# Two halves of weights at a time for keys, queries, both gates and the linear attention's output product

## The reference, cut to what matters

```
q, k, v, g, a_lr, p, bg = split(h @ w_in)     # h: 256 x 2048, for the latent tokens and for the context
o   = gla(q, k, v, decay(a_lr))               # 4 heads, forward and backward, chunks of 64
y1  = (rms(o) * gain * silu(g)) @ w_gla_out   # 256 x 2048 by 2048 x 2048
y2  = pool_branch(p) @ w_pool_out
x   = x + gt * ((sigmoid(bg1) * y1 + sigmoid(bg2) * y2) @ w_out)
```

## Time and profile before

| | |
|---|---|
| median of three runs | 2921.17 us |
| span of the profiled execution | 2918.2 us |
| its device time beside the span | not noted; the runs' median is 3.0 us above the span |
| TensorE busy | 2884.3 us (99%) |
| VectorE busy | 2112.9 us (72%) |
| ScalarE busy | 1444.3 us (49%) |
| TensorE's granted clock over the span | 0.996 of full |
| HBM read | 639.58 MB |

### The profile page before, as it was taken

One profiled execution on the slowest core, in us unless ns is written; L12 is line 12 of the kernel. 1 busy time (PEld: TensorE's weight loads), 2 busy tenths in 40 slices (PEclk: granted clock), 3 DMA queues, 4 the chain that ended last, 5 costly groups with the idle time before them and its releaser, 6 DMA issues.

```text
span 2918.2 us, 41112 instructions
## 1 busy us (share of the span) xinstructions
PE 2884.3 (99%) x16696; PEld 2513.1 (86%) x16696; DVE 2112.9 (72%) x2920; ACT 1444.3 (49%) x1929; POOL 10.8 (0%) x25
## 2 busy tenths in 40 slices
PE   8999999999999999999999999999999999999998
PEld 7889989888888888888878888888878888888887
DVE  6566767998998877699767665559987765555557
ACT  5455656544444445465445444544555444444444
POOL 0000000000000000000000000000000000000000
PEclk9999999999999999999999999999999999999999
DMA  7555345777777885587745455678647765555553
GB/s 272 188 213 191 131 169 207 267 267 260 268 267 262 317 304 203 200 296 279 270 167 199 175 184 197 219 262 292 241 155 284 291 220 188 188 188 189 187 188 114
DMA packets 108252, 653.78 MB, mean 224 GB/s; under 512 B 12032, under 2 KB 12288, under 8 KB 43936
## 3 DMA queue, kind: packets, MB, share of 16 engines
q1 hardware_dynamic: 100800, 625.93, 58.8%
q10 hardware_dynamic: 5328, 17.83, 1.5%
q0 software_dynamic: 1936, 7.41, 0.7%
HBM read 639.58 MB, written 11.53 MB: 223 GB/s over the span
## 4 chain that ended last, share of the span: by engine, by line
PE 95%; DVE 3%; ACT 1%; issue 1%; DMA 0%; SPq 0%; ACTq 0%; DVEq 0%
PE PS L527 51%; PE PS L538 27%; PE PS L613 3%; PE PS L615 3%; PE PS L623 3%; PE PS L522 1%; PE PS L524 1%; DVE RL L2162 1%; PE PS L870 1%; PE PS L1114 0%; PE PS L1128 0%; PE PS L645 0%; PE PS L839 0%; DVE X L3146 0%; PE PS L1046 0%
## 5 line engine op out<-in xcount | busy, mean ns | idle before, releaser
L2162 DVE TENSOR_TENSOR RL<-RW,RH 128x1024 fp32r<-128x1024 f32 x974 | 1171.1, 1221 | 424.8 <-ACT RH L1281 420.0
L1281 ACT ACTIVATE RH<-RW 128x1024 fp32r<-128x1024 f32 x974 | 1012.6, 1053 | 640.2 <-PE PS L527 499.5
L527 PE MATMUL PS<-A,RH 128*128 128x512 f32 x4272 | 1045.5, 394 | 13.3 <-ACT RH L1281 8.6
L527 PEld LDWEIGHTS PS<-A,RH 128*128 128x128 f32 x4272 | 782.5, 189 | 167.7 <-ACT RH L1281 8.9
L538 PEld LDWEIGHTS PS<-A,RL 128*128 128x128 f32 x4544 | 594.9, 191 | 28.3
L538 PE MATMUL PS<-A,RL 128*128 128x256 f32 x4544 | 606.6, 283 | 0.0
L527 PE MATMUL PS<-H,RH 128*128 128x512 f32 x2248 | 551.7, 396 | 0.0
L527 PEld LDWEIGHTS PS<-H,RH 128*128 128x128 f32 x2248 | 412.7, 188 | 86.1
L1288 ACT ACTIVATE LT<-PS 128x512 f32<-128x512 f32 x214 | 127.6, 596 | 473.6 <-PE PS L538 473.2
L538 PEld LDWEIGHTS PS<-H,RL 128*128 128x128 f32 x2304 | 296.1, 188 | 14.3
L538 PE MATMUL PS<-H,RL 128*128 128x256 f32 x2304 | 301.2, 282 | 0.0
(11 more groups left out here) (281 smaller groups left out, 1756.2 us busy)
## 6 DMA issues: line engine op xcount, KB each, us to landing
RW<-in_w_fin SPq DMA_DIRECT2D x88, 1024.0 KB, 4.8
G<-in_w_ada SPq DMA_DIRECT2D x160, 512.0 KB, 6.2
RW<-in_w_up SPq DMA_DIRECT2D x64, 1024.0 KB, 4.9
RW<-in_w_down SPq DMA_DIRECT2D x64, 1024.0 KB, 4.9
RW<-in_w_fout SPq DMA_DIRECT2D x44, 1024.0 KB, 4.8
RW<-in_w_v SPq DMA_DIRECT2D x32, 1024.0 KB, 4.8
RW<-in_w_bg SPq DMA_DIRECT2D x32, 1024.0 KB, 4.9
RW<-in_w_k SPq DMA_DIRECT2D x16, 1024.0 KB, 5.4
```

The costliest lines, as they stand in the source:

```text
L527: done = t.matmul(pair[mm][:, :], w, x2(4 * c + k)[0], start=c == 0 and k == 0, stop=False, skip_group_check=True)
L1281: a.activation(m.high(x), m.slot(j)[:, x % 2 * HC:x % 2 * HC + HC], ACT.Copy).then_inc(s["hi"], 1)
L2162: v.tensor_tensor(m.low(x), m.slot(j)[:, x % 2 * HC:x % 2 * HC + HC], m.high(x).bitcast(F32), ALU.subtract).then_inc(s["lo"], 1)
```

## The change

In four calls of `gemm` on the tensor engine, `paired=True` is added. No other engine's program and no data layout changes.

```
-    L.k2 = lambda use, b0, nb: gemm(nb, 4, A2, modulated(use) if use == b0 == 0 else nothing)
-    L.q2 = lambda: gemm(4, 4, A2, modulated(1), zipped=True)
+    L.k2 = lambda use, b0, nb: gemm(nb, 4, A2, modulated(use) if use == b0 == 0 else nothing, paired=True)
+    L.q2 = lambda: gemm(4, 4, A2, modulated(1), zipped=True, paired=True)
...
-    L.bg2 = lambda: gemm(4, 4, A2, nothing)
+    L.bg2 = lambda: gemm(4, 4, A2, nothing, paired=True)
...
-    L.gout = lambda: gemm(8, 4, H2, lambda c: t.wait_ge(s["gl"], c + 1))
+    L.gout = lambda: gemm(8, 4, H2, lambda c: t.wait_ge(s["gl"], c + 1), paired=True)
```

## The result

The kernel after takes 2925.39 us (median of 20 runs, 2923.64 to 2927.42), the one before 2920.62 us in the 20 runs beside it (2919.69 to 2921.69). The ratio is 1.0017, 95% interval 1.0011 to 1.0023: +4.8 us. The slowdown is less than the 0.2% that the prediction set as its bound for the same, but the interval doesn't reach 1: twenty runs beside twenty do tell 0.17% from nothing, where the prediction said that a measurement couldn't. The forecast was 2925.0 us.

What follows compares the result with a forecast made beforehand. TensorE, busy 99% of the span, was taken as the bound. The terms -1.1 + 0 + 0.95 + 4.1 + 0 - 0.1 gave +3.8 us on a median of 2921.17: 2925.0 us, range 2920.3 to 2929.5.

Steps and rivals of the forecast that it cites:

- Part 1: Keys, queries and gates, A as moving operand: pairing saves 0.020 us a pair, -1.1 us for 56 pairs.
- the order would cost nothing: Rival, all four products: pairs save nothing, waits stay; +4.9 us, 2926.1 us, chance 0.08.
- Part 2: gout's 16 pairs, H as moving operand: the order alone changes 0 us, bounds -0.3 and +0.1 us.
- Part 3: Queries' start: the second half's wait for ScalarE's copy grows by a half's narrow part, +0.95 us, bounds 0 and +1.6.
- Part 4: gout beside the pool: B directly follows A and waits for ScalarE's copy; +1.0 us a window, +4.1 us for four.
- The clock is no further price: TensorE's added waits: no extra cost from the clock, since it was 1.00 over the stretch with the 1.6 us wait.
- Part 5: Heads: some steps come a half, 2.8 us, later; one return to the product less in the fourth head, -0.1 us.
- the tight place: Fourth head's output, whose norm must be done before the transposes: nothing gained or lost, bounds 0 and +0.4 us.
- Part 6: Weights feeding the pairs: wanted 0.94 us sooner; narrowest behind gout's gate reload, 2.3 us of cover left, cost 0.
- ScalarE late in the pool: Rival, pool: ScalarE not idle when A's bank is full; +4.2 us (2929.2) or +6.6 us (2931.6), chance 0.10.
- The reload: Rival, gout's gate reload: it outlasts its cover and TensorE loses 2 us or so; 2927 to 2931 us, chance 0.04.
- The wait in the pool: Rival, pool: no wait, as A and B aren't side by side or the copy is early; 2920.3 us, chance 0.08.

Runs made afterwards that it cites:

- e8: Against the kernel before: keys and gates paired, queries paired from their second pair on, gout single; 2919.35 us against 2920.43, ratio 0.9997.
- e7: The kernel before with 120 pairs of other products (both MLPs and g2) unpaired; 2922.77 us against 2920.43, ratio 1.0007.
- e4: The kernel after with the eight wide matmuls of the queries' first half issued twice; 2924.67 us against 2920.30 for the kernel before, ratio 1.0015.
- e5: The kernel before with seven of eight narrow matmuls of the queries' first half left out; 2921.99 us against 2920.43, ratio 1.0003.
- e9: The kernel before with seven of eight wide and seven of eight narrow matmuls of the queries' first half left out; 2923.06 us against 2920.38, ratio 1.0008.
- e10: The kernel before with four of eight wide and seven of eight narrow matmuls of the queries' first half left out; 2922.02 us against 2920.38, ratio 1.0006.
- e1: The kernel after with the queries unpaired again; 2923.03 us against 2920.30 for the kernel before, ratio 1.001.
- e2: The kernel after with gout unpaired again; 2921.77 us against 2920.30 for the kernel before, ratio 1.0004.
- e6: The kernel after with the pool's lane one slot later on every engine; 2923.83 us against 2920.43 for the kernel before, ratio 1.001.

## Why the prediction was right or wrong

The total was right within 1 us. One term was missing, the clock's, and the small gains of parts 1 and 5 were taken too large; all of these made the sum too low.

- **Part 1, pairs with A: right in kind, somewhat too large.** Forecast -1.1 us for 56 pairs. Measured in e8: -0.15 for the queries' last seven pairs (0.021 each), -0.67 for the 40 behind the second low rank, -0.12 for the context's eight, some -0.9 in all. Where nothing lies between, a pair gives 0.020 (e7); beside the heads and the context's steps it gives less, 0.017 and 0.015. The price of a matmul by its columns, which the prediction quotes from the Trainium skill ("TensorE: Matmul & The Clock Gate", section "Back-to-back issue gap"), is called there that of an isolated matmul; for a stream with weight loads the section gives 131 ns for 512 columns, further still from the 228 ns here. That the order would cost nothing was the prediction's reading of that price. The runs refute it: g2 in e7 is 0.32 us slower in single halves, and the stretches with pairs are 0.12, 0.15 and 0.65 us shorter.
- **Part 2, pairs with H: right.** The kernel after has gout's last eleven pairs behind the pool, with no step between; here are the first of them and pout's first:

```profile
1955.89 3.88 PE L527 MATMUL PS<-H,RH 128*128 128x512 f32 x16
...
2017.74 2.46 PE L527 MATMUL PS<-A,RH 128*128 128x512 f32 x10
```

They take 61.85 us, 5.623 us a pair, against 5.621 for two single halves before. So pairing gout gains nothing where it can be seen by itself.
- **Part 3, the queries' start: the wait right (+0.96, 1.59 to 2.55), the price wrong.** The term was +0.95 and measured +2.42 + 0.16 = +2.6 us in the profiled execution. The failed step is the one that closes part 4, "The clock is no further price". It took a stretch with a 1.6 us wait as evidence for one of 2.55. Filling the stand took back 1.58 us of the stretch (e4), and a longer stand in the kernel before, without any new pair, brought a cost of the kind (e5, e9, e10). On average over executions the price is less than in the profile: e1, which undoes the wait and the clock together, gives back 2.0 us of medians.
- **Part 4, the pool: right, step by step.** It measured 2.66, 1.64 and 10.11 us against 2.64, 1.65 and 10.09, and +4.01 in the stretch against +4.1. (The prediction's own rows give 4 x (10.09 - 9.08) = 4.04, so the +4.1 is rounded up.) e2 takes away all of it.
- **Part 5, the heads: the tight place right, the small gain wrong.** The norm kept its place in the timeline after, VectorE first, then TensorE:

```profile
1774.45 1.41 DVE L2966 TENSOR_SCALAR G<-PS,SM 128x512 f32<-128x512 f32 x2 [0.71 <-ACT SM L1962]
```

```profile
1764.08 1.88 PE L1128 MATMUL PS<-G 128*128 128x512 f32 x4
...
1776.50 1.04 PE L1144 MATMUL PS<-C,G 128*128 128x128 f32 x8
```

VectorE ends at 1775.86, 0.64 us before the transposes, where the earlier trace rows had 0.65, and L1144 has no wait. The -0.1 us for steps side by side was not there: before, L1103 took 0.47 us to the product behind it; after, 0.55 to L1114. e6 shows the same in the pool.
- **Part 6, what feeds the pairs: right.** No kernel shows a wait of L527 or L538 for weights in these four products. The gates' reload held ScalarE 8.56 us after, 8.35 before.
- **The basis.** I took the median as 3.0 us above the span. The profiled execution after took 2925.28 us with a span of 2924.0, so 1.3 us lie around it, and the trace of before, at 2918.2, was of a quick execution. That is why the spans differ by 5.8 and the medians by 4.8. The forecast, a difference added to the median, was not hurt by that.
- **The rivals.** ScalarE late in the pool needed steps closer than the change puts them (e6). The reload stayed covered. The wait in the pool was there four times.
- **Luck.** Against the 2920.62 us beside it the change cost +4.8 us where the sum had +3.8. The forecast came closer than that, 0.4 us, because its base of three runs, 2921.17, lay 0.55 us too high.

## What to carry to other kernels

When two pieces of a product are joined, look at what else was placed between them: here two steps of another lane, the second fed by the first, lost the half of 2.8 us that covered a copy between them, and that cost 4.0 us, four times what the pairs gave. Regroup where no step of another lane loses its cover by it, and take the first pair of a product out if its second piece waits for a bank. A wait of TensorE that grows is to be priced with the half clock behind it, by a row with a wait as long, not by one with a shorter wait.

## What the runs showed of the hardware

- Behind stands of TensorE of 0.7 and 1.6 us at the queries the granted clock stayed at 1.00 in every profile here. At 2.4 us (e5) the times and the recorded clocks speak for a fall in 6 of 11 executions, at 3.3 us (e10) the times for one in 10 of 11, though the one profile of each shows none. At 2.55 us three profiles of three show it (the kernel after, e2, e6), and at 4.0 us the one of e9. A fall cost 1.6 us behind a 2.55 us stand (48.95 against 47.37 us in e4) and 2.4 us behind the one of 4.0 us.
- Sixteen wide and sixteen narrow matmuls in two groups are 0.020 us quicker than in four with A as the moving operand (5.567 against 5.587 us), and no quicker with H (5.623 against 5.621), where sixteen wide ones take 1959.61 - 1955.89 = 3.72 us in place of 3.65.
- After a step of small float32 matmuls whatever follows takes 0.1 to 0.2 us more, be it the product (3.00 against 2.81 us behind A in the earlier trace rows) or another such step (B to A 1.73 against 1.54 us in e6).
